# Weight products of a two-block network read and written from the last column to the first

## The chip, the cores and the metric

The kernel runs on one core of a Trainium2 chip. The metric is the device time of one execution in microseconds (us). For the kernel before there are three runs, 1978.68, 1980.60 and 1981.69 us, with the median 1980.6 us; the profile comes from one further execution.

## The reference, cut to what matters

Two blocks are computed on an activation `x` of 256 tokens by 2048 features in fp32. The first block is a gated convolution layer followed by a gated linear recurrence layer (HGRN), the second is one sliding-window attention layer with a SwiGLU feed-forward part. Seen from this change, what matters is that each layer begins and ends with a large product of an activation by a weight matrix:

```python
def conformer_conv(h, w_in, dw, dw_b, ln_g, ln_b, w_out):
    u = h @ w_in                      # 2048 x 6144
    ...
    return (v * jax.nn.silu(z)) @ w_out   # 2048 x 2048

def hgrn2_mixer(h, w_in, lb_fwd, lb_bwd, o_norm, w_out):
    u = h @ w_in                      # 2048 x 10240
    ...
    return (o * jax.nn.silu(z)) @ w_out   # 2048 x 2048

def sliding_window_attention(h, positions, w_qkv, q_norm, k_norm, sinks, w_o):
    qkv = h @ w_qkv                   # 2048 x 2560
    ...
    return out.reshape(b, s, ATT_Q_HEADS * ATT_HEAD_DIM) @ w_o   # 2048 x 2048

def swiglu(h, w_gate, w_up, w_down):  # 2048 x 5632 twice, 5632 x 2048
    return (jax.nn.silu(h @ w_gate) * (h @ w_up)) @ w_down
```

## The kernel before, in words

**One stream of weight chunks.** All weight matrices are cut into chunks of 256 rows by 512 columns (`CK` = 2 tiles of 128 rows, `GC` = 512 columns, 512 KB in fp32). Ten phases follow one another (`phases`, lines 117 to 126): `conv_ab`, `conv_z`, `conv_out`, `hgrn`, `hgrn_z`, `hgrn_out`, `kv_q`, `att_out`, `gate_up`, `down`. Together they have 656 chunks. A chunk passes through one of four slots: the queue of SyncE loads it into `raw` (line 338), ScalarE copies it to `w_hi` in the type float32r (line 707), and VectorE writes the rest `w_lo = raw - w_hi` (line 1101; for some chunks GpSimd does, lines 389 and 398). The semaphores `raw_in`, `hi_ready`, `split_ready` and `chunk_used` link these steps; ScalarE fills a slot of `w_hi` again once the product that used it four chunks ago has increased `chunk_used`.

**The products.** For each chunk TensorE multiplies the activation, which is split in the same way into a high and a low part, by the chunk (`stream` in the TensorE block, lines 412 to 438). The stationary operand is a 128x128 tile of the activation (`hi` or `lo`), the moving operand is one row tile of the chunk, 128 partitions by 512 columns, and the result goes to one PSUM bank of the accumulator `acc`, whose 512 fp32 columns it fills. For each of two row tiles `kk` and two token blocks `tb` there are three matmuls, high by high, high by low and low by high (lines 427 to 429), so twelve for a chunk. They all add to the same 512 columns for eight chunks (22 in `down`). In the last chunk of the kernel the four (`kk`, `tb`) pairs come in another order, so that the first token block is done earlier. Moving columns are read from column 0 to column 511, and the accumulator's columns are written in the same order. `acc` has two pairs of banks, used in turn.

**What stands around the products.** ScalarE (line 716) and VectorE (lines 1129 and 1520) read a finished accumulator and release its pair through `pair_free`. Between chunks, at places written out by hand as hooks, TensorE runs the smaller matmuls of the layers: transposes (line 409), the levels of the recurrence (lines 542 and 550), scores and mixing in attention (lines 622, 624, 636, 647), and sums for a norm. These are plain fp32, go to the other PSUM tensor `T`, and read and write their columns forwards. Line 542 runs 128x128 blocks, with 128 moving columns. On VectorE, lines 1299 to 1302 work on halves of blocks whose width goes down from 64 to 1 (`halves`, `LEVELS`); at width 1 every second fp32 element is read and written.

Of the kernel before, what the change touches and what calls it, by code (L numbers as in the profile page):

```python
# [34 lines left out]
P = 128  # L35
# [118 lines left out]
def build(nc, t, out):  # L154
    ph = phases()
    ctx = ExitStack()
    with ctx:
        def sb(stack, name, shape, dt=F32):
            return stack.enter_context(nc.sbuf_tensor(name, shape, dt))
# [6 lines left out]
        w_hi = sb(ctx, "w_hi", [P, SLOTS, CK, GC], F32R)  # L166
        w_lo = sb(ctx, "w_lo", [P, SLOTS, CK, GC], F32R)
# [84 lines left out]
        acc = ctx.enter_context(nc.psum_tensor("acc", [P, 2, TB, GC], F32))  # L252
# [53 lines left out]
        def slots(base, i):  # L306

            return base + i, i % SLOTS, base * (16 // SLOTS) + 16 * (i // SLOTS + 1)
# [94 lines left out]
        def _(pe):  # L403
# [8 lines left out]
            def stream(name, j, hi, lo, hooks=None, need=None):  # L412

                p = ph[name]
                base = p.base(j)
                for i, (k, c) in enumerate(p.seq):
                    n, slot, _ = slots(base, i)
                    if need is not None and k == 0:
                        need(c)
                    if c == 0 and not (isinstance(p.use(j, k), int) and p.use(j, k) == 0):  # L420
                        pe.wait_ge(pair_free[p.pair(k)], 2 * p.use(j, k))
                    pe.wait_ge(split_ready, n + 1)
                    ends = name == "down" and i == len(p.seq) - 1
                    for kk, tb in ((0, 0), (1, 0), (0, 1), (1, 1)) if ends else ((0, 0), (0, 1), (1, 0), (1, 1)):
                        kt = c * CK + kk
                        o, a = acc[:, p.pair(k), tb, :], slice(tb * P, (tb + 1) * P)
                        nc.tensor.matmul(o, hi[:, kt, a], w_hi[:, slot, kk, :], start=kt == 0, stop=False)  # L427
                        nc.tensor.matmul(o, hi[:, kt, a], w_lo[:, slot, kk, :], start=False, stop=False)  # L428
                        last = nc.tensor.matmul(o, lo[:, kt, a], w_hi[:, slot, kk, :], start=False,  # L429
                                                stop=kt == p.chunks * CK - 1)  # L430
                        if ends and (kk, tb) == (1, 0):
                            last.then_inc(half_done, 1)
                        if (kk, tb) == (0, 1):
                            for f in (hooks or {}).get(i - 0.5, ()):
                                f()
                    last.then_inc(chunk_used, 1)
                    for f in (hooks or {}).get(i, ()):
                        f()
# [29 lines left out]
            def ab(j):  # L468
                if is_first(j):
                    stream("conv_ab", j, h_hi, h_lo, None, normed(0))  # L470
                else:
                    stream("conv_ab", j, h_hi, h_lo, Hooks().put(2 if is_first(j - 1) else 4, lambda: v_turn(j - 1)))
# [43 lines left out]
            for q in range(4):  # L516
                at.put((26, 27, 27.5, 28)[q], lambda q=q: variance(q))
            at.put(28.5, fold_variance)
            stream("conv_z", 0, h_hi, h_lo, at)
            stream("conv_out", 0, y_hi, y_lo, x_turns("conv_out", 1, (c_zc, 8)).put(1, lambda: z_turn(3)),  # L520
                   lambda c: pe.wait_ge(c_lo, c + 1))
# [1068 lines left out]
```

## Time and profile before

| what | value |
|---|---|
| median of the runs (lowest, highest) | 1980.6 us (1978.68, 1981.69) |
| profiled execution, its own time | 1978.78 us |
| its span, first to last instruction | 1977.0 us |
| mean granted TensorE clock | 0.999 |
| instructions in the span | 26937, of them 9924 matmuls |
| HBM read | 349.07 MB, 178 GB/s over the span |

The profiled execution takes 1.78 us more than its span, and lies 1.8 us under the median. In the rows, PE is TensorE's matmul side, PEld its loading of stationary tiles, DVE is VectorE, ACT ScalarE, POOL GpSimd. L427 is line 427 of the kernel. The duration of a matmul in a row reaches from its start to its modelled end and overlaps the next one, so the pace of TensorE is read from the distance between two starts and not from the durations.

### The profile page before, as it was taken

How to read it: one execution, taken by the hardware profiler on the slowest of the kernel's cores; microseconds unless marked ns; L12 is line 12 of the kernel's file. 1: busy time of each engine (PE TensorE's matmuls, PEld its weight loads, DVE VectorE, ACT ScalarE, POOL GpSimd, SP SyncE). 2: the span in 40 equal slices, each digit the busy share in tenths (PEclk: the TensorE clock that was granted, in tenths of full speed). 3: DMA queues.
4: the chain of work that ended last, by engine and by line, in shares of the span. 5: the costliest groups of instructions: out<-in, count | busy, mean ns of one | idle time of the engine just before them, and what ended most of it. 6: DMA issues, size and time to landing. Idle time of an engine off the chain costs nothing.

```text
span 1977.0 us, 26937 instructions
## 1 busy us (share of the span) xinstructions
PE 1949.7 (99%) x9924; PEld 1601.0 (81%) x9924; DVE 1247.7 (63%) x1799; ACT 1083.0 (55%) x1430; POOL 220.6 (11%) x99
## 2 busy tenths in 40 slices
PE   8999999999999999999999999999999999999999
PEld 6888878888888788778887778888888888888887
DVE  5699976544868687786567885554445444444443
ACT  6444465546768585975456775544344444443332
POOL 0899840000000000000000100000000000000000
PEclk9999999999999999999999999999999999999999
DMA  8665645565545455545555444665656656556654
GB/s 305 193 188 178 189 153 188 172 211 169 162 149 161 139 176 153 159 129 180 172 186 158 136 129 159 206 189 191 190 170 194 198 189 192 186 190 196 195 192 160
DMA packets 183004, 352.45 MB, mean 178 GB/s; under 512 B 11776, under 2 KB 12288, under 8 KB 182912
## 3 DMA queue, kind: packets, MB, share of 16 engines
q1 hardware_dynamic: 181488, 350.68, 56.1%
q8 instruction: 59, 0.97, 0.2%
q10 hardware_dynamic: 1424, 0.53, 0.1%
q14 instruction: 33, 0.27, 0.0%
HBM read 349.07 MB, written 2.10 MB: 178 GB/s over the span
## 4 chain that ended last, share of the span: by engine, by line
PE 94%; ACT 2%; DVE 2%; issue 1%; ACTq 0%; DMA 0%; DVEq 0%
PE acc L427 29%; PE acc L429 29%; PE acc L428 29%; PE T L409 2%; PE T L550 2%; DVE w_lo L1101 1%; ACT w_hi L707 1%; PE T L647 1%; PE T L636 1%; PE T L563 0%; PE T L542 0%; PE T L562 0%; PE T L624 0%; ACTq L717 0%; PE T L622 0%
## 5 line engine op out<-in xcount | busy, mean ns | idle before, releaser
L1101 DVE TENSOR_TENSOR w_lo<-raw,w_hi 128x1024 fp32r<-128x1024 f32 x568 | 689.9, 1223 | 638.6 <-ACT w_hi L707 631.5
L707 ACT ACTIVATE w_hi<-raw 128x1024 fp32r<-128x1024 f32 x656 | 683.7, 1058 | 520.8 <-PE acc L429 493.5
L427 PE MATMUL acc<-w_hi,h_hi 128*128 128x512 f32 x1888 | 746.7, 395 | 15.8 <-DVE w_lo L1101 15.6
L428 PE MATMUL acc<-w_lo,h_hi 128*128 128x512 f32 x1888 | 736.5, 390 | 0.0
L429 PE MATMUL acc<-w_hi,h_lo 128*128 128x512 f32 x1888 | 736.5, 390 | 0.0
L427 PEld LDWEIGHTS acc<-w_hi,h_hi 128*128 128x128 f32 x1888 | 355.2, 188 | 95.6 <-issue 14.2
L429 PEld LDWEIGHTS acc<-w_hi,h_lo 128*128 128x128 f32 x1888 | 355.1, 188 | 74.9
L428 PEld LDWEIGHTS acc<-w_lo,h_hi 128*128 128x128 f32 x1888 | 355.5, 188 | 71.0
L389 POOL TENSOR_TENSOR w_lo<-raw,w_hi 128x1024 fp32r<-128x1024 f32 x80 | 190.1, 2404 | 79.3 <-ACT w_hi L707 79.0
L1163 DVE SCALAR_TENSOR_TENSOR T<-vpad,feat,T 128x256 f32<-128x256 f32 x464 | 182.5, 484 | 0.0
L427 PE MATMUL acc<-w_hi,y_hi 128*128 128x512 f32 x384 | 152.3, 397 | 3.0 <-DVE y_lo L1106 2.6
L428 PE MATMUL acc<-w_lo,y_hi 128*128 128x512 f32 x384 | 149.5, 389 | 0.0
L427 PE MATMUL acc<-w_hi,f_hi 128*128 128x512 f32 x352 | 137.0, 389 | 0.0
L429 PE MATMUL acc<-w_hi,f_lo 128*128 128x512 f32 x352 | 137.0, 389 | 0.0
L428 PE MATMUL acc<-w_lo,f_hi 128*128 128x512 f32 x352 | 136.9, 389 | 0.0
L398 POOL TENSOR_TENSOR w_lo<-raw,w_hi 128x1024 fp32r<-128x1024 f32 x8 | 19.1, 2384 | 862.6 <-ACT w_hi L707 862.3
L429 PE MATMUL acc<-w_hi,hy_lo 128*128 128x512 f32 x256 | 99.9, 390 | 0.0
L427 PEld LDWEIGHTS acc<-w_hi,y_hi 128*128 128x128 f32 x384 | 72.1, 188 | 19.7 <-DVE y_lo L1106 3.6
L428 PEld LDWEIGHTS acc<-w_lo,y_hi 128*128 128x128 f32 x384 | 72.2, 188 | 14.2
L913 ACT ACTIVATE E<-E 128x2048 f32<-128x2048 f32 x28 | 53.7, 1917 | 43.1 <-DVE E L1302 43.0
L427 PEld LDWEIGHTS acc<-w_hi,f_hi 128*128 128x128 f32 x352 | 66.1, 188 | 13.8
L429 PEld LDWEIGHTS acc<-w_hi,f_lo 128*128 128x128 f32 x352 | 66.1, 188 | 13.8
(214 smaller groups left out, 1320.9 us busy)
## 6 DMA issues: line engine op xcount, KB each, us to landing
raw<-in_hgrn_w_in_dram SPq DMA_DIRECT2D x160, 512.0 KB, 3.6
raw<-in_conv_w_in_dram SPq DMA_DIRECT2D x96, 512.0 KB, 3.6
raw<-in_ffn_w_gate_dram SPq DMA_DIRECT2D x88, 512.0 KB, 4.3
raw<-in_ffn_w_up_dram SPq DMA_DIRECT2D x88, 512.0 KB, 4.1
raw<-in_ffn_w_down_dram SPq DMA_DIRECT2D x88, 512.0 KB, 3.8
raw<-in_attn_w_qkv_dram SPq DMA_DIRECT2D x40, 512.0 KB, 3.7
raw<-in_conv_w_out_dram SPq DMA_DIRECT2D x32, 512.0 KB, 4.5
raw<-in_hgrn_w_out_dram SPq DMA_DIRECT2D x32, 512.0 KB, 4.7
```

The source lines that it names most:

```text
L389: nc.gpsimd.tensor_tensor(w_lo[:, slot, :, :], raw[:, slot, :, :], rounded(w_hi[:, slot, :, :]), ALU.subtract).then_inc(split_ready, 1)
L409: last = nc.tensor.transpose(dst[:, q // 2, at:at + P], src[:, tb, q * P:(q + 1) * P], ident[:, :])
L427: nc.tensor.matmul(o, hi[:, kt, a], w_hi[:, slot, kk, :], start=kt == 0, stop=False)
L428: nc.tensor.matmul(o, hi[:, kt, a], w_lo[:, slot, kk, :], start=False, stop=False)
L429: last = nc.tensor.matmul(o, lo[:, kt, a], w_hi[:, slot, kk, :], start=False, stop=kt == p.chunks * CK - 1)
L550: last = nc.tensor.matmul(T[i * HB:(i + 1) * HB, 2 + s % 2, (2 * h + b) * HB:(2 * h + b + 1) * HB], g, q, start=True, stop=True)
L636: last = nc.tensor.transpose(T[:, h % 2, b * P:(b + 1) * P], sm[:, h, (b + 1) * P:(b + 2) * P], ident[:, :])
L647: last = nc.tensor.matmul(o, v(tb), w, start=tb == 0, stop=tb == 1)
L707: A(w_hi[:, slot, :, :], raw[:, slot, :, :], ACT.Copy).then_inc(hi_ready, 1)
L913: A(e, e, ACT.Exp).then_inc(g_E, 1)
L1101: TT(w_lo[:, slot, :, :], raw[:, slot, :, :], rounded(w_hi[:, slot, :, :]), ALU.subtract).then_inc(split_ready, 1)
L1163: STT(out=cy[:, kt, :] if tap == TAPS - 1 else y, in0=v, scalar=w, in1=y, op0=ALU.mult, op1=ALU.add).then_inc(c_tap, 1)
```

## The change

The slices of the moving operand (`w_hi`, `w_lo`) and of the accumulator get a step of -1 over the 512 columns. All three matmuls of all 656 chunks are concerned, in every phase. The stationary operands, the number of instructions, their order and all semaphores stay, and so do the matmuls into `T`. Column 511 of the weights still lands in column 511 of the accumulator.

```diff
-                        o, a = acc[:, p.pair(k), tb, :], slice(tb * P, (tb + 1) * P)
-                        nc.tensor.matmul(o, hi[:, kt, a], w_hi[:, slot, kk, :], start=kt == 0, stop=False)
-                        nc.tensor.matmul(o, hi[:, kt, a], w_lo[:, slot, kk, :], start=False, stop=False)
-                        last = nc.tensor.matmul(o, lo[:, kt, a], w_hi[:, slot, kk, :], start=False,
+                        o, a = acc[:, p.pair(k), tb, ::-1], slice(tb * P, (tb + 1) * P)
+                        nc.tensor.matmul(o, hi[:, kt, a], w_hi[:, slot, kk, ::-1], start=kt == 0, stop=False)
+                        nc.tensor.matmul(o, hi[:, kt, a], w_lo[:, slot, kk, ::-1], start=False, stop=False)
+                        last = nc.tensor.matmul(o, lo[:, kt, a], w_hi[:, slot, kk, ::-1], start=False,
                                                 stop=kt == p.chunks * CK - 1)
```

## Rows read from the trace of the kernel before

**Rows 1.** The page: busy time of the engines, and the granted clock in 40 slices.

```profile
PE 1949.7 (99%) x9924; PEld 1601.0 (81%) x9924; DVE 1247.7 (63%) x1799; ACT 1083.0 (55%) x1430; POOL 220.6 (11%) x99
...
PEclk9999999999999999999999999999999999999999
```

**Rows 2.** The page: the chain that ended last, by engine and line.

```profile
PE 94%; ACT 2%; DVE 2%; issue 1%; ACTq 0%; DMA 0%; DVEq 0%
PE acc L427 29%; PE acc L429 29%; PE acc L428 29%; PE T L409 2%; PE T L550 2%; DVE w_lo L1101 1%; ACT w_hi L707 1%; PE T L647 1%; PE T L636 1%; PE T L563 0%; PE T L542 0%; PE T L562 0%; PE T L624 0%; ACTq L717 0%; PE T L622 0%
```

**Rows 3.** The waits of TensorE, all of them.

```profile
PE acc L427 <- DVE w_lo L1101: 16.1, 7, 9.8
PE T L550 <- DVE E L1308: 4.7, 3, 3.0
PE acc L427 <- DVE y_lo L1106: 2.6, 1, 2.6
```

**Rows 4.** TensorE's groups by line and shape: busy us, mean ns | idle before.

```profile
L427 PE MATMUL acc<-w_hi,h_hi 128*128 128x512 f32 x1888 | 746.7, 395 | 15.8 <-DVE w_lo L1101 15.6
L428 PE MATMUL acc<-w_lo,h_hi 128*128 128x512 f32 x1888 | 736.5, 390 | 0.0
L429 PE MATMUL acc<-w_hi,h_lo 128*128 128x512 f32 x1888 | 736.5, 390 | 0.0
L427 PE MATMUL acc<-w_hi,y_hi 128*128 128x512 f32 x384 | 152.3, 397 | 3.0 <-DVE y_lo L1106 2.6 <-DVE w_lo L1101 0.4
...
L427 PE MATMUL acc<-w_hi,f_hi 128*128 128x512 f32 x352 | 137.0, 389 | 0.0
```

**Rows 5.** TensorE's timeline at 1000 us: start, duration, line (13 starts in all).

```profile
999.97 0.39 PE L429 MATMUL acc<-w_hi,h_lo 128*128 128x512 f32 x1
1000.20 0.39 PE L427 MATMUL acc<-w_hi,h_hi 128*128 128x512 f32 x1
1000.42 0.39 PE L428 MATMUL acc<-w_lo,h_hi 128*128 128x512 f32 x1
...
1002.69 0.39 PE L429 MATMUL acc<-w_hi,h_lo 128*128 128x512 f32 x1
```

**Rows 6.** TensorE's timeline from its first matmul, 9 to 16.5 us.

```profile
9.81 0.76 PE L427 MATMUL acc<-w_hi,h_hi 128*128 128x512 f32 x1 [9.81 <-DVE w_lo L1101]
10.37 0.63 PE L428 MATMUL acc<-w_lo,h_hi 128*128 128x512 f32 x1
10.80 0.63 PE L429 MATMUL acc<-w_hi,h_lo 128*128 128x512 f32 x1
11.23 0.63 PE L427 MATMUL acc<-w_hi,h_hi 128*128 128x512 f32 x1
...
14.21 0.63 PE L428 MATMUL acc<-w_lo,h_hi 128*128 128x512 f32 x1
14.64 0.44 PE L429 MATMUL acc<-w_hi,h_lo 128*128 128x512 f32 x1
14.91 0.40 PE L427 MATMUL acc<-w_hi,h_hi 128*128 128x512 f32 x1
15.15 0.39 PE L428 MATMUL acc<-w_lo,h_hi 128*128 128x512 f32 x1
15.38 0.40 PE L429 MATMUL acc<-w_hi,h_lo 128*128 128x512 f32 x1
```

**Rows 7.** TensorE's timeline at 511 us, where line 542 runs 128 moving columns.

```profile
511.03 1.95 PE L542 MATMUL T<-E 128*128 128x128 f32 x16
512.73 0.48 PE L427 MATMUL acc<-w_hi,h_hi 128*128 128x512 f32 x1
513.05 0.40 PE L428 MATMUL acc<-w_lo,h_hi 128*128 128x512 f32 x1
```

**Rows 8.** Single lines of VectorE: duration ns min/median/max, first and last start.

```profile
L1302 DVE TENSOR_TENSOR E<-Bc x28: 681/685/691, 505.1 to 884.8; 128x512 f32<-128x512 f32 x28
L1202 DVE TENSOR_TENSOR cy<-cy,szt x8: 678/685/686, 285.8 to 306.4; 128x512 f32<-128x512 f32 x8
```

**Rows 9.** ScalarE's and VectorE's longest groups: busy us, mean ns | idle before.

```profile
L707 ACT ACTIVATE w_hi<-raw 128x1024 fp32r<-128x1024 f32 x656 | 683.7, 1058 | 520.8 <-PE acc L429 493.5 <-issue 10.9 <-DMA raw<-in_conv_w_in_dram 7.9
L1101 DVE TENSOR_TENSOR w_lo<-raw,w_hi 128x1024 fp32r<-128x1024 f32 x568 | 689.9, 1223 | 638.6 <-ACT w_hi L707 631.5 <-issue 2.6
```

## The prediction

> **What bounds the kernel now.** I read the page's busy times first: TensorE is busy for 1949.7 us of 1977.0 us at full granted clock, the next engine for 63% [rows 1]. A busy engine need not be the bound, so the chain that ended last comes next: 94% of it is TensorE, and the three lines of the weight products hold 87% [rows 2]. TensorE waits for another engine for 16.1 + 4.7 + 2.6 = 23.4 us in the whole kernel, of which 9.8 us are the start, before the first chunk is there [rows 3]. The time is therefore the number of weight products times their pace, plus the smaller matmuls between them.
>
> The number: line 427 has 1888 + 384 + 352 = 2624 matmuls, and lines 428 and 429 as many each, so 7872 [rows 4], which is 12 for each of 656 chunks. The pace is not in their mean duration of 390 ns, because they overlap; it is the distance of starts. From 999.97 to 1002.69 us there are 12 steps, 2.72 / 12 = 0.2267 us each [rows 5]. So 7872 x 0.2267 = 1784.6 us of the span, 90%, lie in exactly the instructions that the change rewrites, and none of it is covered by other work. ScalarE and VectorE stand behind them: ScalarE sits idle 493.5 us until a product releases its slot, and VectorE 631.5 us until ScalarE has delivered [rows 9].
>
> At 2.4 GHz, 512 columns at one column a cycle would take 213.3 ns. The step measured is 226.7 ns, so 13.4 ns a matmul are not columns. I keep this number: it is all that an order of columns could ever give back while each matmul streams 512 columns, 7872 x 13.4 ns = 105 us.
>
> **The change part by part.** It removes and adds no instruction, no byte, no wait and no DMA. Three things differ for each of the 7872 matmuls.
>
> - *The moving operand is read backwards.* No row shows TensorE doing this. If the read port takes fp32 columns one by one, or keeps a small group of neighbours that it has fetched, a step of -1 costs what +1 costs. The nearest row for a step other than +1 is on VectorE: line 1302 works on halves of blocks with widths from 64 down to 1, so its 28 instructions include four in which every second element is read and written, and all 28 lie between 681 and 691 ns. Line 1202, with contiguous operands and the same 512 elements, has a median of 685 ns, as has line 1302 [rows 8]. That engine is slower than a column in 0.42 ns and its step is still upwards, so the row excludes little; but where this case shows a step at all, the step is free. I take 0 ns.
> - *The accumulator is written backwards.* Each write adds to what the bank holds. Every matmul of a group runs in the same direction, so a matmul begins at column 511 when its predecessor on the same bank ends at column 0: the distance between writing a column and writing it again is one matmul, as before. I take 0 ns.
> - *What follows.* The readers of the accumulator wait for the end of the whole matmul (`chunk_used`), not for a column, so it does not matter which column is finished last. The same holds for ScalarE, which overwrites a slot of `w_hi` when the chunk is used up. Transposes and the other matmuls into `T` stay forward and use other banks; nothing of theirs is touched. I take 0 us for all three.
>
> Bounds of the unknown price, per matmul. Downwards: -13.4 ns, the whole rest over the column time; nothing in the rows ties this rest to the direction, so I give this end next to nothing. Upwards: half the column rate. The trace shows this rate twice. The first weight products start 0.43 us apart (10.37, 10.80, 11.23 us) and fall to 0.23 us only after 14.9 us [rows 6]; 0.427 us is 512 columns at 1.2 GHz, the lower of the two clock levels, though the granted clock reads full there too. And line 542, plain fp32, has 16 matmuls of 128 columns in 512.73 - 511.03 = 1.70 us, 0.83 ns a column or 0.425 us for 512 [rows 7], in a stretch in which the products around it run at the full level. So TensorE can be limited to a column every 0.83 ns by something other than its clock. The upper end is thus 0.427 - 0.227 = +0.200 us a matmul. Between ends so far apart I take 0, since the row nearest to the change (a non-unit step at the same element size) shows 0.
>
> **The sum.** 1978.8 us (the profiled execution; span 1977.0 and 1.8 around it) + 7872 x 0 = 1978.8 us. It lies 1.8 us under the median of the runs, so the forecast for the median is 1980.6 us. One ns more a matmul is worth 7.9 us, as there is hardly a wait that would absorb it (23.4 us in all, and most of these belong to starts that move along). What a measurement of this kernel can tell from no change is about 0.2%, 4 us, or half a ns a matmul.
>
> **The rivals.**
>
> *Half rate, slower by far.* The port that reads the moving columns, or the one that writes the accumulator, serves two neighbouring fp32 columns together, and only for an ascending pair; a descending one gets one column each 0.83 ns. Place: each of the 7872 matmuls. Price: +0.200 us each, 7872 x 0.200 = +1574 us, giving about 3555 us. It decides as soon as pairing depends on the sign, and not at all otherwise; there is no middle. For it: line 542 shows that a slower column pace exists at the full clock [rows 7]. Against it: the pair (511, 510) holds the same two neighbouring words as (510, 511), and the start at column 511 splits no such pair. Chance 0.14.
>
> The Trainium skill has the rule for this. "PSUM — Partial Sum Buffer", section Specifications, says of PSUM that it has 8-byte lines and that any non-contiguous access pattern slows matmuls significantly; "Advanced Engine Details and Errata", section Memory Cachelines, words it as every two consecutive elements having to be contiguous. Read by the letter of the first, a step of -1 is not contiguous and the sum would be this rival's; read by the second, two consecutive columns still share a line and the sum is mine. No trace of before shows a matmul written with any other step than +1, so it stays untested.
>
> *A fixed price for each matmul.* Setting up a descending pattern costs some ns at the beginning of each matmul. The row that prices such overheads is the rest over the columns, 13.4 ns; as much again for each would be +105 us, 2086 us; a third of it +35 us, 2016 us. For it: the rest exists, and it is the same in early and late stages. Against it: it can as well belong to the change of the stationary tile, which stays. Chance 0.10, with more weight near zero.
>
> *A small gain.* The reverse order meets the writes of ScalarE, VectorE and the DMAs elsewhere, and a part of the 13.4 ns vanishes: 1 ns each is -7.9 us, 1973 us. No row shows that this rest depends on such traffic. Or the median simply falls a little. Chance 0.05.
>
> *The change does nothing at all*, because the lowering turns two descending patterns of one instruction back into ascending ones. That would be 1980.6 us as well; it is contained in the forecast, and only the trace's operand patterns or a run with one operand reversed could tell them apart.
>
> **How the numbers follow.** Forecast of no price: 0.71, of which 0.69 within 0.2% and 0.01 on either side. Half rate 0.14 and fixed price 0.10 are slower, 0.25, with the 0.01 above: 0.26. The small gain and the other 0.01 give faster 0.06; rounded, faster 0.05, same 0.69, slower 0.26. The range shall leave out at most 0.2: the half rate (0.14) stays out as it lies alone at 3555 us, then I can spare 0.04 of the fixed price, everything above 5 ns a matmul, 1980.6 + 39 = 2020 us, and 0.02 of the gains, below 1972 us. The range is 1972 to 2020 us.
>
> **What would show it.** Right: starts of weight products 0.2267 us apart, 7872 of them, TensorE busy for about 1950 us and its waits near 23 us; ScalarE's wait for the products near 494 us. Half rate: starts 0.427 us apart at a granted clock of full, durations near 0.6 us, ScalarE and VectorE mostly idle. Fixed price: starts a few ns further apart and equal in all stages, with line 542 unchanged. The prediction is wrong if the distance of starts moves by over half a ns, or if the first product after a transpose, which changes the direction of writing, is clearly later than before.

## The result, and the profile after

The changed kernel takes 2025.01 us (median of 4 runs, 2024.54 to 2026.69), the kernel before 1980.39 us beside it. The ratio is 1.0226, with a 95% interval of 1.0214 to 1.0238: slower by 44.6 us. I had forecast 1980.6 us and a range up to 2020 us.

The page of the changed kernel: busy times, granted clock, and the chain that ended last by engine:

```profile
PE 1998.8 (99%) x9924; PEld 1604.8 (79%) x9924; DVE 1247.8 (62%) x1799; ACT 1082.5 (54%) x1430; POOL 218.8 (11%) x99
...
PEclk9999999999999999999999999999999999999999
...
PE 96%; DVE 1%; ACT 1%; issue 1%; DMA 0%; ACTq 0%; DVEq 0%
```

The number of instructions is the same as in [rows 1], the clock is granted in full, and TensorE's busy time has grown by 49.1 us. VectorE and ScalarE are as busy as before (1247.8 and 1082.5 us). TensorE's share of the chain rises from 94% in [rows 2] to 96%. All of the loss is in TensorE.

Its waits, to be set beside [rows 3]:

```profile
PE acc L427 <- DVE w_lo L1101: 14.5, 5, 9.5
PE T L550 <- DVE E L1308: 2.9, 1, 2.9
PE acc L427 <- DVE y_lo L1106: 2.6, 1, 2.6
```

They sum to 20.0 us, where [rows 3] gave 23.4. Nobody new holds TensorE up; it waits a little less, as its partners have more time.

The pace, from TensorE's timeline at 1400 us (start, duration, line):

```profile
1399.67 0.40 PE L429 MATMUL acc<-w_hi,h_lo 128*128 128x512 f32 x1
1399.90 0.40 PE L427 MATMUL acc<-w_hi,h_hi 128*128 128x512 f32 x1
1400.14 0.40 PE L428 MATMUL acc<-w_lo,h_hi 128*128 128x512 f32 x1
...
1402.47 0.40 PE L429 MATMUL acc<-w_hi,h_lo 128*128 128x512 f32 x1
```

Twelve steps from 1399.67 to 1402.47 us: 2.80 / 12 = 0.2333 us, against 0.2267 us in [rows 5]. That is 6.7 ns, or 16 cycles at 2.4 GHz, on each matmul. The groups by line and shape say the same in another form, mean durations of 398 ns for 390 in [rows 4], and ScalarE's wait for a product grows from 493.5 us in [rows 9] to 526.8 us:

```profile
L707 ACT ACTIVATE w_hi<-raw 128x1024 fp32r<-128x1024 f32 x656 | 683.3, 1057 | 551.5 <-PE acc L429 526.8
L427 PE MATMUL acc<-w_hi,h_hi 128*128 128x512 f32 x1888 | 761.7, 403 | 14.6 <-DVE w_lo L1101 14.5
L428 PE MATMUL acc<-w_lo,h_hi 128*128 128x512 f32 x1888 | 752.0, 398 | 0.0
```

The account closes. 7872 x 6.7 ns would be 52 us. But the kernel before did not keep 0.2267 us everywhere: for some matmuls after an interruption it ran at the slower step (in [rows 6], 15.15 to 15.38 and 14.91 to 15.15 us are 0.23 and 0.24 us). By the starts in its trace, the first three steps after a break average 231 to 233 ns, and from the tenth on about 226.7 ns. Averaged over all distances under 0.3 us between two neighbouring products, some 7600 of them in each trace, the pace goes from 0.2271 to 0.2334 us, 6.2 ns. 7872 x 6.2 ns = 49.0 us, less 3.4 us of shorter waits, gives 45.6 us; the span grew by 2022.7 - 1977.0 = 45.7 us.

### The profile page after: what moved, and what is told of

It reads as the page before. It is cut to its first block, busy times and chain, and to the rows that moved or that the text cites. A ratio compares the mean times of both kernels' runs of the same rounds, so it can differ in the third digit from the quotient of the medians.

```text
span 2022.7 us, 26937 instructions
## 1 busy us (share of the span) xinstructions
PE 1998.8 (99%) x9924; PEld 1604.8 (79%) x9924; DVE 1247.8 (62%) x1799; ACT 1082.5 (54%) x1430; POOL 218.8 (11%) x99
## 4 chain that ended last, share of the span: by engine, by line
PE 96%; DVE 1%; ACT 1%; issue 1%; DMA 0%; ACTq 0%; DVEq 0%
PE acc L427 30%; PE acc L428 30%; PE acc L429 30%; PE T L409 2%; PE T L550 2%; PE T L647 1%; PE T L636 1%; DVE w_lo L1101 1%; ACT w_hi L707 0%; PE T L563 0%; PE T L562 0%; PE T L542 0%; PE T L624 0%; PE T L622 0%; DMA norm<-in_norm_dram 0%
## 5 line engine op out<-in xcount | busy, mean ns | idle before, releaser
L707 ACT ACTIVATE w_hi<-raw 128x1024 fp32r<-128x1024 f32 x656 | 683.3, 1057 | 551.5 <-PE acc L429 526.8
L427 PE MATMUL acc<-w_hi,h_hi 128*128 128x512 f32 x1888 | 761.7, 403 | 14.6 <-DVE w_lo L1101 14.5
L428 PE MATMUL acc<-w_lo,h_hi 128*128 128x512 f32 x1888 | 752.0, 398 | 0.0
L429 PE MATMUL acc<-w_hi,h_lo 128*128 128x512 f32 x1888 | 751.8, 398 | 0.0
L428 PEld LDWEIGHTS acc<-w_lo,f_hi 128*128 128x128 f32 x352 | 66.2, 188 | 16.0
```

Source lines behind the costliest of these rows:

```text
L427: nc.tensor.matmul(o, hi[:, kt, a], w_hi[:, slot, kk, ::-1], start=kt == 0, stop=False)
L428: nc.tensor.matmul(o, hi[:, kt, a], w_lo[:, slot, kk, ::-1], start=False, stop=False)
L707: A(w_hi[:, slot, :, :], raw[:, slot, :, :], ACT.Copy).then_inc(hi_ready, 1)
```

## The experiments

### Which operand: one of the two directions at a time

Neither kernel of this section computes the reference: the columns of its products come out mirrored. Against the changed kernel, once only the accumulator's slice is turned back:

```diff
-                        o, a = acc[:, p.pair(k), tb, ::-1], slice(tb * P, (tb + 1) * P)
+                        o, a = acc[:, p.pair(k), tb, :], slice(tb * P, (tb + 1) * P)
```

and once only the three slices of the moving operand are, which leaves the accumulator alone backwards:

```diff
-                        nc.tensor.matmul(o, hi[:, kt, a], w_hi[:, slot, kk, ::-1], start=kt == 0, stop=False)
-                        nc.tensor.matmul(o, hi[:, kt, a], w_lo[:, slot, kk, ::-1], start=False, stop=False)
-                        last = nc.tensor.matmul(o, lo[:, kt, a], w_hi[:, slot, kk, ::-1], start=False,
+                        nc.tensor.matmul(o, hi[:, kt, a], w_hi[:, slot, kk, :], start=kt == 0, stop=False)
+                        nc.tensor.matmul(o, hi[:, kt, a], w_lo[:, slot, kk, :], start=False, stop=False)
+                        last = nc.tensor.matmul(o, lo[:, kt, a], w_hi[:, slot, kk, :], start=False,
```

Expected of the moving operand alone:

> Weight products read backwards and written forwards: the columns of each group of 512 come out mirrored, so the values after the first product are not the reference's; the number, size and order of all instructions stay. The changed kernel has weight products start 0.2333 us apart where the kernel before has 0.2267, and takes 2025 us. Theory R (reading): the 6.7 ns belong to the moving operand that is read from its last column: 0.2333 us apart, about 2025 us. Theory W (writing): they belong to the accumulator written downwards: 0.2267 us apart, about 1980 us. Theory B (both): each costs a part, or a mirrored pair costs more than either: a distance between the two, or above 0.2333.

Expected of the accumulator alone:

> Weight products read forwards and written backwards (mirrored results again, same instructions). Theory R: 0.2267 us apart, about 1980 us. Theory W: 0.2333 us apart, about 2025 us. Theory B: between the two or above 0.2333.

Measured: moving alone 2024.58 us, ratio 1.022 (1.0203 to 1.0237); accumulator alone 1980.36 us, ratio 1.0003 (0.9993 to 1.0012). The timelines at 1400 us, first of the moving operand alone, then of the accumulator alone:

```profile
1400.30 0.40 PE L428 MATMUL acc<-w_lo,h_hi 128*128 128x512 f32 x1
1400.53 0.40 PE L429 MATMUL acc<-w_hi,h_lo 128*128 128x512 f32 x1
...
1402.86 0.40 PE L427 MATMUL acc<-w_hi,h_hi 128*128 128x512 f32 x1
```

```profile
1400.37 0.39 PE L428 MATMUL acc<-w_lo,h_hi 128*128 128x512 f32 x1
1400.59 0.39 PE L429 MATMUL acc<-w_hi,h_lo 128*128 128x512 f32 x1
...
1402.86 0.39 PE L427 MATMUL acc<-w_hi,h_hi 128*128 128x512 f32 x1
```

Eleven steps take 2.56 us in the first (0.2327) and 2.49 us in the second (0.2264), within the rounding of two starts 0.2333 and 0.2267. So theory R holds for the whole price, and theory W has none of it: writing a PSUM bank from its last column to its first is free. The rule of the Trainium skill that non-contiguous accumulators slow matmuls ("PSUM — Partial Sum Buffer", Specifications) does not reach a step of -1 here; two neighbours still come together, whichever is first.

### TensorE alone: is it direction, address or size?

The kernel loads one tile of weights and of x, copies both to float32r, and then runs stretches of 48 matmuls, each stretch in one form. `N` is 48; two of the stretches stand for the rest:

```python
            for i in range(N):
                last = M(acc[:, 0, :], h[:, i % 16, :], w[:, i % 2, 0:512], start=i == 0, stop=i == N - 1)
            for i in range(N):
                last = M(acc[:, 0, :], h[:, i % 16, :], w[:, i % 2, 0:512][:, ::-1], start=i == 0, stop=i == N - 1)
```

> TensorE alone, 22 stretches of 48 matmuls back to back, each stretch in one form; none of the reference is computed, the output is a copy of x. What is read is the distance of starts in a stretch. The second stretch is the form of the kernel before, the third that of the changed one. If the pace of the kernels is TensorE's own, they show 0.2267 and 0.2333 us; if it comes from the traffic of the other engines, both are the same and nearer 0.2160. Stretches 4 and 5 reverse the moving operand or the accumulator alone: theory R wants the extra 6.7 ns in 4, theory W in 5. Stretches 6 to 8 read forwards from column 1, 2 and 4, stretches 9 and 10 backwards from column 512 and 515: theory A (the alignment of the first column, not the direction) wants the extra in 6 and 7 and not in 8, and another value in 9 than in 10; theory R wants 6 to 8 equal to 2 and 9, 10 equal to 4. Stretches 11 and 12 use two banks in turn, 13 and 14 do not accumulate: if the extra comes from adding to a bank just written, it is gone there. Stretches 15 to 18 have 384 and 256 columns, forwards and backwards: a fixed price stays 6.7 ns, a price by the column falls to 5.0 and 3.3 ns. Stretches 19 to 22 are bfloat16 (forwards, both backwards, moving alone, accumulator alone): a price of lines read from SBUF halves with the bytes or vanishes, a price of the pattern's direction in itself stays.

TensorE's timeline, one row for a stretch (start of the first matmul, time to the modelled end of the last): forwards, both backwards, moving alone, accumulator alone, and forwards from column 1 and from column 2 (the last row's stretch ends where the next begins, at 94.33 us).

```profile
26.77 11.36 PE L58 MATMUL acc<-w,h 128*128 128x512 f32 x48
37.97 11.36 PE L60 MATMUL acc<-w,h 128*128 128x512 f32 x48
49.17 11.37 PE L62 MATMUL acc<-w,h 128*128 128x512 f32 x48
60.37 11.34 PE L64 MATMUL acc<-w,h 128*128 128x512 f32 x48
71.55 11.60 PE L66 MATMUL acc<-w,h 128*128 128x512 f32 x48
82.99 11.50 PE L68 MATMUL acc<-w,h 128*128 128x512 f32 x48
```

A stretch's pace is the distance to the next stretch's start over 48. Forwards (37.97 - 26.77) / 48 = 0.2333 us, the same as both backwards and moving alone; accumulator alone is 0.2329. Neither of the two readings of the expectation fits: without any other engine at work, plain forwards was as slow as backwards, and neither was near 0.2160. A start that is not on 16 bytes made it worse (column 1: 0.2383, column 2: 0.2363), and one that is moved on by a whole 16 bytes did not (column 4: 0.2321). Backwards over the same columns as column 1 took 0.2367, as column 4 0.2335. So theory A has a part of the truth, but it does not explain the change, whose columns begin on 16 bytes. In bfloat16 backwards cost nothing (0.2158 us, moving alone or both, and forwards (211.35 - 201.20) / 47 = 0.2160; there 47 matmuls of 48 are on record). Two banks in turn (0.2327) and no accumulation (0.2329) changed nothing either, so the 13.4 ns beyond 512 columns are not a matter of adding to a bank just written.

What differed from the kernels was where the tensors lay (by the addresses of the built programs). In the kernels, every moving and every stationary operand of the products begins at byte 128 of a 512-byte block; in this run the tensors began at bytes 256 (moving) and 448 (stationary), and the second moving tile lay another 64 bytes on. The next run put them as the kernels have them and then moved one against the other.

> TensorE alone, 31 stretches of 48 float32r matmuls, none of the reference computed, the output is a copy of x. Here the moving and the stationary tensor both begin at byte 128 of a 512-byte block, as the operands of the weight products do; in the first run of forms they did not (bytes 256 and 448), and forwards and backwards took 0.2333 us alike. Read is the mean distance of starts. Stretches 2, 3: forwards, backwards. 4 to 10 shift the stationary tile by 64, 128, ... 448 bytes, moving operand forwards; 11 to 17 the same, backwards. 18, 19: one stationary tile for all; 20, 21: one moving tile for all; 22 to 26: moving operand shifted by 16, 32, 64, 256, 512 bytes forwards; 27, 28: by 64, 256 backwards; 29, 30: 64 stationary columns; 31: two banks in turn. Theory M (meeting: the extra is a loss between the reads of the moving operand and of the next stationary tile, which start together, and depends on where in a block of addresses each is): 2 takes 0.2267 and 3 0.2333 us; some of 4 to 10 rise to 0.2333 or more, at least one of 11 to 17 falls to 0.2267; 26 equals 2. Theory D (direction by itself costs the moving operand 6.7 ns): 11 to 17 are all 0.2333, every forward stretch on a 64-byte boundary is 0.2267. Theory Q (the pace of 0.2267 comes from the traffic or order of the whole kernel, not from addresses): 2 is 0.2333, as in the first run of forms.

Its timeline: forwards, backwards, then forwards with the stationary tile moved on by 64, 128, 192, 256 and 320 bytes.

```profile
25.51 11.04 PE L63 MATMUL acc<-w,h 128*128 128x512 f32 x48
36.39 11.37 PE L65 MATMUL acc<-w,h 128*128 128x512 f32 x48
47.59 11.37 PE L67 MATMUL acc<-w,h 128*128 128x512 f32 x48
58.80 11.32 PE L69 MATMUL acc<-w,h 128*128 128x512 f32 x48
69.96 11.16 PE L71 MATMUL acc<-w,h 128*128 128x512 f32 x48
80.95 11.06 PE L73 MATMUL acc<-w,h 128*128 128x512 f32 x48
91.86 11.36 PE L75 MATMUL acc<-w,h 128*128 128x512 f32 x48
```

Forwards is now (36.39 - 25.51) / 48 = 0.2267 us and backwards (47.59 - 36.39) / 48 = 0.2333 us, both paces of the kernels to the last digit. Theory Q is out. A shift of the stationary tile by 64 bytes takes the forward read to 0.2335, by 128 to 0.2325, by 192 to 0.2290, by 256 back to 0.2273 us. A shift of the moving operand by 16, 32 and 64 bytes gives 0.2319, 0.2331 and 0.2292, by 256 and 512 bytes 0.2273 and 0.2267. So theory D is out as well: forwards by itself is not fast. Its other half came true: backwards stayed at 0.2333 for every shift by a multiple of 64 bytes, so theory M does not hold as written either. One stationary tile or one moving tile for all 48 changed nothing (0.2271 forwards, 0.2333 backwards). With only 64 stationary columns, though, the forward read was slower at the same place, 0.2302.

### The same in the whole kernel

The edit, made once to the kernel before and once to the changed kernel:

```diff
         x = sb(ctx, "x", [P, TB, D])
+        sb(ctx, "shift", [P, 16])
         h_hi = sb(ctx, "h_hi", [P, KT, S], F32R)
```

> The kernel before, all forwards, with 64 bytes put in ahead of h_hi, so that every stationary operand (h, y and f, high and low) begins at byte 192 of a 512-byte block instead of 128 and the moving weights stay at 128; nothing else. Theory M: as in the stretch of TensorE alone (0.2335 us), starts about 0.2333 us apart and about 2025 us, as slow as the changed kernel, without any direction changed. Theory D (direction alone matters in the kernel): 0.2267 us and 1980 us.

> The changed kernel, all backwards, with the same 64 bytes ahead of h_hi. From the stretches of TensorE alone, where backwards took 0.2333 us whatever the shift of the stationary tile: 0.2333 us and about 2025 us, no difference from the changed kernel. A theory in which backwards only moves the best alignment elsewhere would have it at another value than 2025 us.

Measured: forwards with the 64 bytes 2024.55 us, ratio 1.0227 (1.021 to 1.0244); backwards with them 2025.32 us, ratio 1.0233 (1.0216 to 1.025). TensorE's timeline of the first (lines are one further down, 428 is 427 of before):

```profile
1400.33 0.39 PE L429 MATMUL acc<-w_lo,h_hi 128*128 128x512 f32 x1
1400.56 0.39 PE L430 MATMUL acc<-w_hi,h_lo 128*128 128x512 f32 x1
...
1402.89 0.39 PE L428 MATMUL acc<-w_hi,h_hi 128*128 128x512 f32 x1
```

2.56 us for eleven steps again. Sixteen unused words ahead of a tensor, no direction changed, and the kernel is as slow as the changed one. The fast pace of the kernel before is a property of how its two operands lie to each other; the change loses it in another way, and the two losses do not add. By the starts in the two traces they do not look alike either: the changed kernel's steps are an even 233 and 234 ns, those of the shifted one are mostly 231 and 236 ns.

### A third of the matmuls

Against the kernel before:

```diff
-                        nc.tensor.matmul(o, hi[:, kt, a], w_lo[:, slot, kk, :], start=False, stop=False)
+                        nc.tensor.matmul(o[:, ::-1], hi[:, kt, a], w_lo[:, slot, kk, ::-1], start=False, stop=False)
```

> The kernel before with the matmul of line 428 alone (2624 of 7872) reading and writing backwards; results are the same. If the price belongs to each backwards matmul by itself: 6.7 ns each less the share that was absorbed in the whole change (44.6 of 52.5 us arrived), so 0.85 x 17.5 = 14.9 us, about 1995 us, with one step in three at 0.2333 us. If it lies in the change of direction between a matmul and its neighbour, two borders per three matmuls would give about twice that, about 2010 us. If a run of backwards matmuls is needed (a state that builds up), about 1981 us.

Measured: 1993.41 us, ratio 1.0071 (1.0054 to 1.0088), 13.8 us more than the kernel before beside it. The expectation for a price of each backwards matmul by itself was 14.9 us. It is 5.3 ns for each of 2624, beside 5.7 ns for each of 7872 in the change. The trace puts it at the right place: averaged over all its distances under 0.3 us, the step that begins with a matmul of line 428 is 232.4 ns, where it is 227.1 ns in the kernel before, and the steps of the two other lines are 226.9 and 227.7 ns. Neither the border between directions nor a run of them matters.

### What in "backwards" costs: words, lines or blocks

The moving operand was taken in groups: `m(i).rearrange("p (a b) -> p a b", b=4)[:, ::-1, :]` reads groups of 4 columns (16 bytes) from the last to the first, forwards inside; `[:, :, ::-1]` reads the groups in order and each backwards inside.

> TensorE alone, 33 stretches of 48 matmuls, nothing of the reference, the output is a copy of x; operands at byte 128 of a 512-byte block. 2, 3: forwards 0.2267, backwards 0.2333 us as before. 4 to 10: stationary tile shifted by 16, 32, 48, 80, 112, 240, 272 bytes, forwards; 11 to 13: by 16, 32, 240, backwards. 14, 15: 32 stationary columns, 16, 17: the upper 64. 18 to 23: 384, 256 and 448 moving columns, forwards and backwards. 24 to 30: the moving columns in groups: groups of 4 taken backwards but read forwards inside, forwards with each read backwards inside; the same for 16; groups of 64 backwards; groups of 256 backwards, and each backwards inside. 31: every second column. 32, 33: plain fp32, forwards and backwards. Theory M (meeting of the moving read with the read of the next stationary tile): with 32 stationary columns the extra shrinks well below 6.7 ns; it is fixed in the number of moving columns (6.7 at 448, 384, 256). Theory L (lines: the order of lines or of words within a line costs): groups of 4 backwards (lines of 16 bytes) show which of the two by themselves: lines backwards 0.2333 with words forwards, or the reverse; 32 stationary columns change nothing. Theory E (the ends: where the read begins decides): groups of 256 backwards cost as a shift does, and 28, 24, 26 differ with the address of the first column only.

Timeline: groups of 4 backwards, words in them backwards; the same two for 16; groups of 64 backwards, of 256 backwards, each of 256 backwards inside; every second column; plain fp32.

```profile
251.49 11.37 PE L107 MATMUL acc<-w,h 128*128 128x512 f32 x48
262.70 11.06 PE L109 MATMUL acc<-w,h 128*128 128x512 f32 x48
273.59 11.36 PE L111 MATMUL acc<-w,h 128*128 128x512 f32 x48
284.79 12.96 PE L113 MATMUL acc<-w,h 128*128 128x512 f32 x48
297.59 11.07 PE L115 MATMUL acc<-w,h 128*128 128x512 f32 x48
308.50 11.04 PE L117 MATMUL acc<-w,h 128*128 128x512 f32 x48
319.38 11.37 PE L119 MATMUL acc<-w,h 128*128 128x512 f32 x48
330.58 21.93 PE L121 MATMUL acc<-w,h 128*128 128x512 f32 x48
352.33 41.38 PE L123 MATMUL acc<-raw,xr 128*128 128x512 f32 x96
```

Groups of 4 in descending order with ascending words take (262.70 - 251.49) / 48 = 0.2335 us, the words alone descending 0.2269. Turning the 16-byte lines costs, turning the words in one does not. Groups of 64 columns descending take 0.2273, of 256 descending 0.2267. So a read that runs downwards in blocks of 256 bytes is fast. Groups of 16 with each descending inside, which jumps up by 31 columns from group to group, was the slowest of these, 0.2667.

Two parts of the expectation failed. Theory M wanted less extra with 32 stationary columns: backwards stayed at 0.2333, and forwards rose to 0.2317. And the extra is not a constant: from the stretches of this and the last run,

| moving columns | 512 | 480 | 448 | 384 | 320 | 256 |
|---|---|---|---|---|---|---|
| forwards, ns | 226.7 | 216.9 | 202.7 | 173.3 | 146.7 | 120.0 |
| backwards, ns | 233.5 | 220.0 | 206.7 | 177.7 | 146.7 | 118.3 |

at 320 columns there is none, and at 256 backwards is the faster one. The best placement depends on the size too: where the tensors lay in the first run of forms, 256 columns forwards took (195.29 - 189.66) / 48 = 0.1173 us, less than the 0.1200 here.

Theory E, that the place where a read begins decides, is not refuted by these groups. Taking groups of b columns from the last moves the first column read to 4b bytes before the end of the tile, and so changes its place in a block of 256 bytes just as a shift of 4b bytes of the stationary tile does. Groups of 16 should then take what a shift of 64 bytes took in the run before (0.2333 and 0.2335), groups of 64 what 256 bytes took (0.2273 both). What speaks against E as the whole truth is a read that goes backwards throughout: with the stationary tile shifted by 240 bytes it should be as fast as unshifted forwards, and it took 0.2367.

The last run fills the map of positions.

> TensorE alone, 30 stretches of 48 float32r matmuls, nothing of the reference, the output is a copy of x. It fills the map: with the earlier runs the stationary tile then stands at every multiple of 16 bytes within 256, forwards (stretches 4 to 9: 96, 144, 160, 176, 208, 224 bytes) and backwards (10 to 18: 48, 80, 96, 112, 144, 160, 176, 208, 224). 19 to 21: groups of 8, 32, 128 columns backwards, forwards inside; 22 to 26: groups of 2, 8, 32, 64, 128 forwards, backwards inside; 27 to 30: 320 and 480 columns, forwards and backwards. Theory M (meeting) asks for forward values from 226.7 to 233.5 ns with the lowest near a shift of 0 or 256 bytes, and for a backward position under 233. Theory L (the order of the 16-byte lines within about 256 bytes, apart from where the stationary tile is): no backward position under 233; groups of 8 and 32 backwards about 233.3, of 128 about 226.7; backwards inside groups of 2 about 226.7, inside 32 to 128 about 233.3.

Timeline: forwards with the stationary tile at 160, 176 and 208 bytes; backwards at 112 and 144 bytes; groups of 8, 32 and 128 backwards; groups of 2 and 8 with words backwards inside.

```profile
69.94 11.36 PE L71 MATMUL acc<-w,h 128*128 128x512 f32 x48
81.14 11.20 PE L73 MATMUL acc<-w,h 128*128 128x512 f32 x48
92.18 11.36 PE L75 MATMUL acc<-w,h 128*128 128x512 f32 x48
...
148.18 11.37 PE L85 MATMUL acc<-w,h 128*128 128x512 f32 x48
159.38 11.52 PE L87 MATMUL acc<-w,h 128*128 128x512 f32 x48
170.74 11.37 PE L89 MATMUL acc<-w,h 128*128 128x512 f32 x48
...
215.70 11.36 PE L97 MATMUL acc<-w,h 128*128 128x512 f32 x48
226.90 11.32 PE L99 MATMUL acc<-w,h 128*128 128x512 f32 x48
238.06 11.06 PE L101 MATMUL acc<-w,h 128*128 128x512 f32 x48
248.96 11.04 PE L103 MATMUL acc<-w,h 128*128 128x512 f32 x48
259.84 11.35 PE L105 MATMUL acc<-w,h 128*128 128x512 f32 x48
271.03 11.36 PE L107 MATMUL acc<-w,h 128*128 128x512 f32 x48
```

All sixteen positions in 256 bytes together, from the three runs, in ns a matmul:

| shift, bytes | 0 | 16 | 32 | 48 | 64 | 80 | 96 | 112 | 128 | 144 | 160 | 176 | 192 | 208 | 224 | 240 |
|---|---|---|---|---|---|---|---|---|---|---|---|---|---|---|---|---|
| forwards | 226.7 | 233.3 | 233.1 | 233.3 | 233.5 | 232.1 | 234.2 | 233.3 | 232.5 | 233.3 | 233.3 | 230.0 | 229.0 | 233.3 | 233.3 | 226.7 |
| backwards | 233.3 | 233.5 | 233.3 | 233.3 | 233.3 | 233.3 | 233.3 | 233.3 | 233.3 | 236.7 | 233.3 | 236.7 | 233.3 | 233.3 | 233.3 | 236.7 |

Forwards has two positions of sixteen at 226.7 ns, and every operand of the kernel before sits on one. Backwards has none under 233.3. The forward row comes back with a shift of 256 bytes more, 227.3 at 256, 233.1 at 320, 232.5 at 384, 229.2 at 448, but not everywhere: 272 bytes took 226.7 ns, and 16 bytes took 233.3. Either the period is longer than 256 bytes there, or the stretch ahead has a say: the one at 272 bytes followed a fast one, the one at 16 bytes a slow one. By the single starts, both hold their pace to the last step, and the one at 240 bytes also followed a slow one and was fast from its second step, so a say of the stretch ahead is the less likely of the two; another order was not tried. The moving operand moved on by 16 bytes, which leaves the stationary tile 16 bytes behind as 240 does, took 231.9 ns and not 226.7. So the distance within 256 bytes is not the whole rule. Groups of 8 descending take 233.3, of 32 232.5, of 128 227.1; words descending inside groups of 2 226.7, and inside 8, which already turns two lines round, 233.1. That is near what theory L asked, except for the groups of 32.

The groups fit theory E better. Descending groups of 8, 32 and 128 move the start of the read by what a shift of 32, 128 and 512 bytes of the stationary tile does; the forward row has 233.1 and 232.5, and for 512 bytes, where everything lies as unshifted, 226.7; the groups took 233.3, 232.5 and 227.1. For 32 even the single steps repeat in the same order as in the stretch shifted by 128 bytes (230, 232, 241, 233, 230, 232, 228 ns), to within 1 ns. So how far the order of lines reaches, within 256 bytes or less, is not shown: each of these groups also moved the start. Shown is that a read which takes all its lines from the last to the first found no fast position among sixteen. Descending groups of 32 with the stationary tile shifted by 128 bytes would have parted the two; that was not run.

Three whole kernels carried this over, each with a helper on both the moving operand and the accumulator, so that the results stay the same:

```diff
+                        turned = lambda v: v.rearrange("p (a b) -> p a b", b=4)[:, ::-1, :]
-                        o, a = acc[:, p.pair(k), tb, :], slice(tb * P, (tb + 1) * P)
-                        nc.tensor.matmul(o, hi[:, kt, a], w_hi[:, slot, kk, :], start=kt == 0, stop=False)
+                        o, a = turned(acc[:, p.pair(k), tb, :]), slice(tb * P, (tb + 1) * P)
+                        nc.tensor.matmul(o, hi[:, kt, a], turned(w_hi[:, slot, kk, :]), start=kt == 0, stop=False)
```

The two other matmuls are changed in the same way. For the words the helper has `b=4` and `[:, :, ::-1]`, for the blocks of 256 bytes `b=64` and `[:, ::-1, :]`.

> The whole kernel, moving weights and accumulator taken in groups of 4 columns (16 bytes) from the last group to the first, but the 4 words of each group forwards. Results are the same. From TensorE alone (233.5 ns): starts 0.2333 us apart and about 2025 us, all of the change's price. If the order of single words mattered, 1980 us.

> The whole kernel, groups of 4 columns from first to last, the 4 words of each group backwards, in moving weights and accumulator alike. Results are the same. From TensorE alone (226.9 ns): 0.2267 to 0.2270 us apart, 1980 to 1982 us, none of the price although every single step but one in four is -1. If the order of single words mattered, about 2025 us; if an accumulator written in steps of -1 and +7 cost more than a plain one, above 1982 us.

> The whole kernel, groups of 64 columns (256 bytes) from the last to the first, the columns within a group forwards. Results are the same. From TensorE alone (227.3 ns): about 0.2273 us apart, 7872 x 0.6 ns = 5 us, about 1984 us. If any read that runs towards lower addresses overall costs 6.7 ns, about 2025 us.

Measured: lines backwards 2024.82 us, ratio 1.0228 (1.021 to 1.0245); words backwards 1980.26 us, 1.0006 (0.9996 to 1.0016); blocks of 256 bytes backwards 1980.33 us, 1.0004 (0.9995 to 1.0014). The timeline of the lines:

```profile
1399.87 0.40 PE L428 MATMUL acc<-w_hi,h_hi 128*128 128x512 f32 x1
1400.11 0.40 PE L429 MATMUL acc<-w_lo,h_hi 128*128 128x512 f32 x1
...
1402.67 0.40 PE L428 MATMUL acc<-w_hi,h_hi 128*128 128x512 f32 x1
```

2.80 us for twelve steps. Taking the 16-byte lines from the last to the first, with no word in them turned, makes the whole price of the change, and an accumulator written in broken order is free again. The blocks came out at about 1 us instead of the 5 us that 0.6 ns a matmul would make: the 0.2273 of the short stretch came from its first seven or so steps, 224 to 236 ns, after which it ran at 226.7 ns to the end, and the kernel's own steps average 227.1 ns as before.

## Why the prediction was wrong

**The bound, the count and the lever: right.** TensorE's 7872 products were the time, one ns on each was worth nearly 7.9 us (44.6 us came for 6.2 ns on average, 7.2 us a ns, the rest absorbed by waits), and no other engine took part. Two slips in the working do not touch the forecast of 1980.6 us. The chances of the two slower rivals add up to 0.24 and not 0.25. And line 542 was read as 16 matmuls of 128 columns, but the program has 8 there (four heads by two blocks), each recorded as two, as the 96 records for 48 plain fp32 matmuls in the run of groups bear out; a column of such a matmul costs 1.66 ns, twice what was written. The accumulator, the readers and the matmuls into `T` cost the 0 that I gave them; line 542 kept its row of 1.95 us for 16.

**The moving operand read backwards, 0 ns: this is the step that failed.** The term measured 6.7 ns where the kernel ran in step, 5.7 ns net. I took 0 because the nearest row for an unusual step was VectorE's, where every second element cost nothing [rows 8]. TensorE itself, reading every second column, takes (352.33 - 330.58) / 48 = 0.4531 us where it takes 0.2267 for contiguous ones: the price of a step on one engine said nothing about the other, which reads more than twice as fast. The sentence that this row "excludes little" was right, and should have led to a wider range and not to a 0.

**The rival with a fixed price for each matmul was the one whose size came**, with its range of 0 to 13.4 ns from the rest over 213.3 ns and the right signs in the profile: starts further apart by a few ns, equal in all stages (233.3 to 233.5 ns on average in every 200 us), line 542 unchanged. It was given 0.10 and cut at 5 ns by the range. Its mechanism did not come: it laid the price on setting up a descending pattern, and patterns that descend within a line or in blocks of 256 bytes cost nothing, and so does a whole backwards read of 320 columns. That its wide range of sizes held the measured one is luck. Two hints that the step is not a constant stood in the rows. In [rows 6] the kernel before has steps of 0.24 and 0.23 us, 0.47 us for two, right after the steps of 0.43 us end, where [rows 5] has 0.2267; so a slower pace with the same operands existed. And the 13.4 ns were called the same in early and late stages and set aside as possibly the stationary tile's, without asking what the two reads of TensorE do to each other. "Fixed" holds for the 512 columns of this kernel alone.

**Half rate did not come** for a step of -1. Its condition, pairing that depends on the sign, is not met on either side: words within a line are free in both directions. It does come for the moving operand at a step of 2. The Trainium skill says of SBUF that full bandwidth needs at least two hits on each 16-byte line, and that each cross to a new line pays a penalty ("SBUF — State Buffer", Specifications). A step of 2 has two hits a line and crosses twice as often, and takes twice the time, 0.4531 us; so two hits are not enough here, and whether the crossings are what costs was not tested.

**What is shown and what stays open.** Shown: the price is the moving operand's alone, it comes with taking the 16-byte lines from the last to the first and not with the words in them, it is the same with all other engines still, and the fast pace of the kernel before exists only for certain positions of the stationary tile against the moving one. Not shown is the mechanism. In the traces the load of the next stationary tile starts with each product (both at 999.97 us in the kernel before, for one), and two reads that collide would fit the forward half of the map; the backward half hardly depends on where the stationary tile is nor on how many of its columns there are. Open is also over how many bytes the order of lines matters, as the groups that asked it moved the start of the read as well. Why 256 columns turn the sign round is open too. No form of 512 columns tried was faster than 226.7 ns in float32r, so there was no version to beat both kernels.

## What to carry to other kernels

When TensorE streams float32r weights back to back, its pace has a fine structure of some 3% that no busy share and no wait shows: read the distance between starts to the ns, divide by the columns, and ask where the rest comes from before touching an operand. Two things to keep: the order of 16-byte lines in the moving operand ascending, and the stationary and the moving tile beginning at the same place in a 256-byte block, a placement that was fast in every test of 128 stationary and 512 moving columns here (with 64 and 32 stationary columns it took 230.2 and 231.7 ns). A new small tensor ahead of either can cost as much as a bad access pattern, so after any change of the layout look at the step again.

## What the runs showed of the hardware that was not expected

- Sixteen unused words ahead of the stationary tensors cost 2.27% (1.021 to 1.0244) of a kernel.
- Writing the accumulator backwards is free (ratio 1.0003), and with it so are groups turned within 16 bytes or in blocks of 256 bytes (1.0006, 1.0004, moving operand and accumulator alike).
- A moving float32r operand with every second column doubles the step to 0.4531 us; one that starts 4 bytes off a 16-byte line takes 0.2383 us, where the same placement without the 4 bytes took 0.2333.
- In bfloat16 the same 512 columns take 0.2158 us backwards, 2.5 ns over the column time, so at the one placement tried most of the rest of 13.4 ns and the price of direction are not there. Plain fp32 takes 0.8588 us forwards (96 matmul records for 48) and about 0.86 backwards.
